# A sixth slot of expert weights, the shared expert inside it, and the first expert unit ahead of its last products

## The chip, the cores and the metric

The kernel runs on one core of one Trainium2 chip. The metric is the device time in microseconds (us) of one execution. All times below are of this one core.

## The reference, cut to what matters

One decoder layer for 256 prompt tokens and 8 sample tokens, 264 tokens in all, model width 1024, everything in fp32. The first half of the layer (an RWKV-7 mixer, a convolution branch, an output projection) is not touched by the change. The second half is a mixture of experts: 64 experts of width 256, of which the router takes 8 for each token, and one shared expert of width 256 that every token goes through.

```python
h = x + mix                                   # mixers, w_out
xf = rmsnorm(h, norm2_g)                      # 264 x 1024
scores = sigmoid(xf @ w_router)               # 264 x 64
gate = top 8 of the biased scores (4 of 8 groups), normalised, times 2.5
routed = sum over e of (silu(xf @ w_gate[e]) * (xf @ w_up[e]) * gate[:, e]) @ w_down[e]
shared = (silu(xf @ ws_gate) * (xf @ ws_up)) @ ws_down
y = rmsnorm(h + routed + shared, normf_g)
```

w_gate, w_up and w_down are 1 MiB for each expert, so 192 matrices of 1 MiB have to be read once; the shared expert's three are 1 MiB each as well.

## The kernel before, in words

After the mixers (until about 440 us) five programs run side by side, one for each engine, and meet at semaphores: `moe_sp` (SyncE issues the weight loads, in order, on one queue), `moe_pe` (TensorE), `moe_act` (ScalarE), `moe_dve` (VectorE) and `moe_pool` (GpSimd, which gathers token rows).

**Weights.** A ring of `NSLOT` = 5 slots at the top of on-chip memory; a slot holds one expert's three matrices. A "load" is one matrix. Expert number n of the order goes to slot n % 5. The shared expert's gate and up matrices are loaded first, into slot 3 (`SHARED_SLOT`), its down matrix into a buffer of its own, `wsd`; expert 3's gate and up are loaded when the shared products that read slot 3 are done (`shg_mm` 4). `moe_sp` (L438 to L474) then goes through the units: after unit u's gate and up products (`h_mm` u+1, here called h1 for unit 0, h4 for unit 3) it issues the gate and up loads of the experts that take the same slots, and after its down products (`yx_mm` u+1) their down loads.

**Units.** The 64 experts are worked through in 26 units, `UNITS = 'PPP' + 'T' + 'TP' * 11`. A P unit has two experts with 64 token slots each, a T unit three: one with 64 slots and two with few tokens, with 32 each. The first six experts are taken as numbered; the others are sorted by their token counts. A unit's 128 token slots are the 128 partitions of its tile `xe`: VectorE compares each token's position in its expert's list with the slot numbers (`match`, L963), TensorE turns that into row numbers (`index`), VectorE hands them over (`fetch_rows`), and GpSimd gathers the rows from DRAM by an indirect DMA (`fetch`, L1173), of 4 KiB for each slot that holds a token; empty slots move nothing. Slots are filled from the first on, so the low partitions of each strip of 64 or 32 are the ones that are filled.

**One unit on TensorE** (L714 to L728): `index(q+3)`; in units 4 to 12 one of the nine pieces of the shared expert's down product, `shared_down` (`DOWN_AT` = 4, `NDOWN` = 9); `gate_up(q)`; `combine(q-1)`, which weighs and adds the results of the unit before; `turn_hidden(q)`; `turn_gates(q)`; `turn(q+1)`, which transposes the gathered rows; `down(q)`. A `shared_down` writes half a PSUM bank, `ps_sd`, that VectorE has to add to `xrow` (`shared_rows`) before the next one may write it, and before `turn_hidden` may write the other half of that bank (`shy_ready`).

**Ahead of unit 0** TensorE interleaves the router's small products with the shared expert's 32 gate and up products (`shared_gate_up`, 128x264 each, k of 8 in four groups), which all come before `gate_up(0)`.

Of the kernel before, what the change touches and what calls it, by code (L numbers as in the profile page):

```python
# [23 lines left out]
ACT = mybir.ActivationFunctionType  # L24
AX = mybir.AxisListType

D = 1024
# [54 lines left out]
def constants():  # L82
# [9 lines left out]
    parts['slot'] = np.tile(np.arange(SLOTS * MAXPASS)[None, :], (128, 1))  # L92
    parts['token'] = p[:, None] + 128 * np.arange(3)[None, :] - NOROW
# [31 lines left out]
def layer_step(nc, A, out, stop=9):  # L125

    ctx = ExitStack()
    with ctx:
# [189 lines left out]
        NSLOT = 5  # L318
        SHARED_SLOT = 3
        NXE, NYE, NIX, NGT = 2, 2, 8, 6  # L320
        ring0 = TOTAL - NSLOT * 3 * 2048
        assert P2.at <= ring0, (P2.at, ring0)
# [7 lines left out]
        scm = E.take(9 * NE)  # L330
        sc, rp, MK = (scm[:, 3 * NE * i:3 * NE * i + 3 * NE].rearrange("p (t e) -> p t e", t=3) for i in range(3))
        PGT = scm[:, 0:NT]
        bi, bm = (E.take(3, NE) for _ in range(2))
# [14 lines left out]
        OHg = E.take(3, 2 * SLOTS)  # L348
# [28 lines left out]
        xeT1 = xeT[0].rearrange("p k n -> p (k n)")[:, 0:KT * SLOTS].rearrange("p (k n) -> p k n", k=KT)  # L377
        hid1 = hid[0][:, 0:2 * SLOTS]
        hT1 = hT[0].rearrange("p j n -> p (j n)")[:, 0:2 * SLOTS].rearrange("p (j n) -> p j n", j=2)
# [50 lines left out]
        DOWN_AT, NDOWN = 4, 9  # L430
# [7 lines left out]
        def moe_sp(sp):  # L438
            for part, n in enumerate(('ws_gate', 'ws_up')):
                load_item(sp, part, SHARED_SLOT, A[n][0])  # L440
            for e in range(3):
                for part in range(3):
                    load_item(sp, part, e, expert_w(part, e))
            load_item(sp, 2, 3, expert_w(2, 3))
# [16 lines left out]
            for u in range(NU_E):  # L461
# [9 lines left out]
                if after:  # L471
                    sp.wait_ge(S['yx_mm'], u + 1)
# [1695 lines left out]
```

## Time and profile before

| | |
|---|---|
| median of 3 runs | 1015.59 us (1015.31 to 1017.05) |
| profiled execution, its own time | 1017.33 us |
| its span, first to last instruction | 1015.5 us |
| mean granted TensorE clock | 0.971 |
| busy: TensorE, its weight loads, VectorE, ScalarE, GpSimd | 92%, 56%, 49%, 23%, 24% |
| read from DRAM | 263.75 MB |
| weight loads of the experts | 192 of 1024 KB |

The span is about 1.8 us shorter than the execution's own time. The 40 slices of the page are 25.4 us each; the expert half begins in the eighteenth. A busy share of the DMA engines near 1.0 means that all 16 of them move data.

### The profile page before, as it was taken

The page shows a single profiled execution, that of the slowest core. Times are in us where ns is not written, and L with a number is a line of the kernel's source. Part 1 is how long each engine was busy: PE and PEld are TensorE (multiplying, and loading weights), DVE is VectorE, ACT ScalarE, POOL GpSimd, SP SyncE. Part 2 cuts the span into 40 slices and gives each one's busy share as a digit, 9 for nine tenths or more (in the row PEclk, how much of TensorE's full clock was granted, in tenths as well). Part 3 has the DMA queues.
Part 4 walks back from the last instruction along what each step waited for, and adds up shares of the span by engine and source line. Part 5 has one row for each costly group of instructions (what it writes and reads, how often), then busy time and mean ns, then how long its engine had stood idle before and what let it go on. Part 6 is the DMA issues. An engine that isn't in the chain of part 4 may idle for free.

```text
span 1015.5 us, 19351 instructions
## 1 busy us (share of the span) xinstructions
PE 931.5 (92%) x7882; PEld 564.9 (56%) x7882; DVE 500.6 (49%) x1040; ACT 232.7 (23%) x483; POOL 243.5 (24%) x281
## 2 busy tenths in 40 slices
PE   4999999999999997779999999999999799899895
PEld 4878877887787777536834344443343234333332
DVE  2148857885787486985623333432323233323225
ACT  3231134113411351254112111111111111111213
POOL 0039904960794099100100000000000000000000
PEclk9999999999999999979999999999999899999989
DMA  8633144214412408139589999999999999999961
GB/s 243 184 125 95 31 125 142 65 44 138 126 55 84 139 2 290 27 140 419 199 361 406 395 419 420 419 420 419 419 420 420 418 415 419 420 414 419 419 282 44
DMA packets 76741, 265.04 MB, mean 261 GB/s; under 512 B 12942, under 2 KB 44240, under 8 KB 51799
## 3 DMA queue, kind: packets, MB, share of 16 engines
q1 hardware_dynamic: 72791, 254.09, 64.5%
q0 software_dynamic: 3856, 9.64, 2.5%
q8 instruction: 65, 1.06, 0.4%
q14 instruction: 29, 0.24, 0.1%
HBM read 263.75 MB, written 5.89 MB: 266 GB/s over the span
## 4 chain that ended last, share of the span: by engine, by line
PE 62%; DMA 23%; DVE 6%; SPq 3%; ACT 3%; issue 2%; DVEq 0%; ACTq 0%
PE bank L1333 60%; DMA big<-in_w_up 22%; SPq L401 2%; ACT big L1630 2%; DMA big<-in_w_in 1%; PE bank L628 1%; DVE big L1920 1%; ACT L1630 1%; DVE big L1977 1%; DVE big L1973 0%; DVE big L897 0%; DVE big L1168 0%; SPq L1228 0%; PE bank L693 0%; DVE big L1983 0%
## 5 line engine op out<-in xcount | busy, mean ns | idle before, releaser
L1333 PE MATMUL bank<-big 64*64 64x64 f32 (+8 forms) x7412 | 872.1, 373 | 61.5 <-DMA big<-in_w_up 27.6
L1333 PEld LDWEIGHTS bank<-big 64*64 64x64 f32 (+4 forms) x7412 | 509.1, 143 | 406.8 <-issue 336.3
L1630 ACT ACTIVATE big<-bank 128x512 f32<-128x512 f32 (+8 forms) x283 | 121.7, 459 | 620.2 <-PE bank L1333 473.7
L1174 POOL DMA_INDIRECT big<-xg,big x26 | 25.9, 995 | 506.4 <-PE bank L628 399.6
L2119 POOL TENSOR_SCALAR big<-big 128x256 f32<-128x256 f32 x120 | 127.0, 1059 | 0.4
L1045 DVE TENSOR_TENSOR big<-big,bank 128x256 f32<-128x256 f32 x26 | 11.0, 422 | 210.3 <-ACT big L1630 210.3
L2131 POOL TENSOR_TENSOR big<-big 128x256 f32<-128x256 f32 x120 | 87.4, 729 | 0.3
L1083 DVE TENSOR_TENSOR big<-big,bank 128x512 f32<-128x512 f32 x104 | 71.5, 688 | 12.7 <-PE bank L1333 11.3
L1920 DVE SCALAR_TENSOR_TENSOR big<-big 128x256 f32<-128x256 f32 x120 | 74.0, 617 | 4.1
L990 DVE TENSOR_SCALAR big<-bank 128x1 uint32<-128x1 f32 x26 | 4.1, 156 | 112.8 <-PE bank L1333 112.5
L1630 ACT ACTIVATE big<-big 128x272 f32<-128x272 f32 (+9 forms) x108 | 49.8, 505 | 42.6 <-DVE big L1855 11.3
L1630 ACT ACTIVATE big<-bank,big 128x272 f32<-128x272 f32 (+2 forms) x53 | 23.8, 475 | 111.6 <-PE bank L1333 111.5
L2115 POOL TENSOR_SCALAR big<-big 128x256 f32<-128x256 f32 x4 | 2.2, 550 | 170.5 <-DVE big L1898 170.5
L1630 ACT ACT_TABLE_LOAD x30 | 38.5, 1283 | 3.8 <-DVE big L912 2.6
L1837 DVE SCALAR_TENSOR_TENSOR big<-bank,big 128x272 f32<-128x272 f32 x26 | 13.0, 498 | 45.5 <-ACT big L1630 45.5
L966 DVE TENSOR_TENSOR big<-big 128x192 f32<-128x192 f32 (+1 forms) x76 | 28.5, 425 | 0.1
L628 PE MATMUL bank<-big 128*128 128x128 f32 x208 | 28.4, 280 | 0.0
L628 PEld LDWEIGHTS bank<-big 128*128 128x128 f32 x208 | 22.3, 141 | 0.5
L1973 DVE TENSOR_TENSOR big<-bank,big 128x512 f32<-128x512 f32 x20 | 13.8, 692 | 16.2 <-PE bank L1333 16.2
L656 PEld LDWEIGHTS bank<-big 128*128 128x128 f32 x52 | 10.1, 195 | 14.1 <-issue 11.9
L1985 DVE TENSOR_TENSOR big<-big,bank 128x512 f32<-128x512 f32 x20 | 13.7, 687 | 4.5 <-PE bank L1333 4.3
L976 DVE TENSOR_TENSOR big<-big 128x192 f32<-128x192 f32 (+1 forms) x38 | 15.4, 431 | 0.9
(156 smaller groups left out, 356.8 us busy)
## 6 DMA issues: line engine op xcount, KB each, us to landing
big<-in_w_gate SPq DMA_DIRECT2D x64, 1024.0 KB, 17.9
big<-in_w_up SPq DMA_DIRECT2D x64, 1024.0 KB, 23.6
big<-in_w_down SPq DMA_DIRECT2D x64, 1024.0 KB, 25.2
big<-in_w_in SPq DMA_DIRECT2D x29, 1024.0 KB, 5.4
big<-in_w_out SPq DMA_DIRECT2D x2, 2048.0 KB, 12.1
big<-in_state_wkv SPq DMA_DIRECT2D x32, 64.0 KB, 2.2
out_wkv_s<-big SPq DMA_DIRECT2D x32, 64.0 KB, 3.9
big<-in_x_prompt SPq DMA_DIRECT2D x2, 512.0 KB, 3.2
```

The costliest lines, as they stand in the source:

```text
L401: sp.dma_start(dst, ap).then_inc(S[('wgu_in', 'wgu_in', 'wd_in')[part] + str(slot)], 16)
L628: ins = nc.tensor.transpose(ps_x[h][:, 128 * (k % 4):128 * (k % 4) + 128], xe[q % NXE][:, 128 * k:128 * k + 128], ident)
L966: ins = v.tensor_tensor(dst[:, :, a:b].rearrange("p t (x n) -> p t x n", x=x), K['slot'][:, first:first + w].unsqueeze(1).unsqueeze(1) .br ...
L976: ins = v.tensor_tensor(view, view, at.unsqueeze(3).broadcast_to([128, 3, x, w]), M)
L1083: note(v.tensor_tensor(x, x, comb_bank(q, n), AD), 'cb_sum')
L1174: pool.indirect_dma_start(out=x[0:n, :], out_offset=None, in_=xg, in_offset=bass.IndirectOffsetOnAxis(ap=idxu[0:n, col:col + 1], axis=0), ...
L1333: return nc.tensor.matmul(out_, lhsT=lhsT, rhs=rhs, start=start, stop=stop)
L1630: return nc.scalar.activation(out_, in_, f, **kw)
L1920: note(v.scalar_tensor_tensor(out=acc, in0=u, scalar=cw, in1=acc, op0=M, op1=AD), 'tap')
L1973: link(v.tensor_tensor(Y_st, bank(0), bc(f'level{m}'), M), 'y_ready')
L2119: note(gp.tensor_scalar(TP[:, w % 3, :], u, cw, None, ALU.mult), 'tapm')
L2131: note(gp.tensor_tensor(acc, acc, TP[:, w % 3, :], ALU.add), 'tapm')
```

## The change

- **Memory.** `NSLOT` is 6 and `SHARED_SLOT` 5. `SLOT_AT` places the slots: 0 to 3 where the old slots 0 to 3 were, 5 where the old slot 4 was, and 4 below all of them, over the end of w_out. The space comes from buffers: `xeT`, `hid` and `hT` are single, `NGT` is 2, `ye[1]` and `xq` lie over `x2T`, `wsd` is the down part of slot 5, `OHg`, `bi` and `bm` share one area.
- **Order of the loads.** Experts 0 to 3 whole; then, after the residual (`h2_ready` 8), the shared gate and up and expert 4; the final norm's row behind these; the shared down after `mk_ready`. After h1: gate and up of experts 6 and 7, then those of expert 5 when the shared products are done; expert 5's down when all nine `shared_down` are done.
- **Order on TensorE.** `gate_up(0)` comes ahead of the last ten shared products. The nine `shared_down` lie in units 0 (pieces 0 to 2), 1 (3 to 7) and 2 (8).
- **Order on VectorE and ScalarE** follows: `fetch_rows(0)` ahead of `order_experts`, `shared_hidden(1)` and `shared_rows` inside `pair(0)` to `pair(2)`.
- **Directions.** A new constant `lane` holds 0 to 63 and then 63 to 0. The second strip of 64 in a P unit and the second strip of 32 in a T unit are filled from the last partition down; the strip of 64 of a T unit is filled upwards in one half of the T units and downwards in the other (`q // 2 % 2`).

```diff
@@ -90,6 +90,8 @@
+    lane = np.arange(SLOTS)
+    parts['lane'] = np.tile(np.concatenate([lane, lane[::-1]])[None, :], (128, 1))
...
-        NSLOT = 5
-        SHARED_SLOT = 3
-        NXE, NYE, NIX, NGT = 2, 2, 8, 6
+        NSLOT = 6
+        SHARED_SLOT = 5
+        SLOT_AT = (1, 2, 3, 4, 0, 5)
+        NXE, NYE, NIX, NGT = 2, 2, 8, 2
         ring0 = TOTAL - NSLOT * 3 * 2048
-        assert P2.at <= ring0, (P2.at, ring0)
+        assert P2.at <= ring0 + 6144, (P2.at, ring0)
...
-        scm = E.take(9 * NE)
+        scm = E.take(15 * NE)
-        bi, bm = (E.take(3, NE) for _ in range(2))
+        bi, bm = (scm[:, 3 * NE * i:3 * NE * i + 3 * NE].rearrange("p (t e) -> p t e", t=3) for i in (3, 4))
...
-        OHg = E.take(3, 2 * SLOTS)
+        OHg = scm[:, 9 * NE:15 * NE].rearrange("p (t n) -> p t n", t=3)
...
-        xeT = [E.take(KT, 2 * SLOTS) for _ in range(2)]
-        hid = [E.take(FE) for _ in range(2)]
-        hT = [E.take(2, 2 * SLOTS) for _ in range(2)]
+        xeT, hid, hT = E.take(KT, 2 * SLOTS), E.take(FE), E.take(2, 2 * SLOTS)
-        ye = [x2p[:, 2, :], E.take(D)]
-        xq = E.take(QD)
-        wsd = E.take(2, D)
-        GT = [x2T.rearrange("p k n -> p (k n)")[:, NT * i:NT * i + NT] for i in range(NGT)]
-        E8 = xeT[1].rearrange("p k n -> p (k n)")[:, 0:8 * NE].rearrange("p (a e) -> p a e", a=8)
+        x2T_flat = x2T.rearrange("p k n -> p (k n)")
+        GT = [x2T_flat[:, NT * i:NT * i + NT] for i in range(NGT)]
+        ye = [x2p[:, 2, :], x2T_flat[:, NGT * NT:NGT * NT + D]]
+        xq = x2T_flat[:, NGT * NT + D:NGT * NT + D + QD]
+        E8 = xeT.rearrange("p k n -> p (k n)")[:, 0:8 * NE].rearrange("p (a e) -> p a e", a=8)
...
-            W_ = Arena(big, ring0 + i * 6144, ring0 + (i + 1) * 6144)
+            W_ = Arena(big, ring0 + SLOT_AT[i] * 6144, ring0 + (SLOT_AT[i] + 1) * 6144)
             slot_w.append((W_.take(2, KT, FE), W_.take(2, D)))
+        wsd = slot_w[SHARED_SLOT][1]
...
-        DOWN_AT, NDOWN = 4, 9
+        NDOWN = 9
...
         def moe_sp(sp):
+            for e in range(4):
+                for part in range(3):
+                    load_item(sp, part, e, expert_w(part, e))
+            sp.wait_ge(S['h2_ready'], 8)
             for part, n in enumerate(('ws_gate', 'ws_up')):
                 load_item(sp, part, SHARED_SLOT, A[n][0])
-            for e in range(3):
-                for part in range(3):
-                    load_item(sp, part, e, expert_w(part, e))
-            load_item(sp, 2, 3, expert_w(2, 3))
-            sp.wait_ge(S['h2_ready'], 8)
+            sp.wait_ge(S['wo_mm'], 3)
             load_item(sp, 0, 4, expert_w(0, 4))
             sp.wait_ge(S['x2_ready'], 3)
-            sp.dma_start(grow, A['normf_g'].rearrange("(a d) -> a d", a=1).partition_broadcast(128)) \
-              .then_inc(S['grow_in'], 16)
             sp.dma_start(xg[0:NP, :].rearrange("(t p) d -> p t d", p=128), x2p[:, 0:2, :]).then_inc(S['x2_out'], 16)
             sp.dma_start(xg[NP:NT, :], x2p[0:NS, 2, :]).then_inc(S['x2_out'], 16)
             load_item(sp, 1, 4, expert_w(1, 4))
+            load_item(sp, 2, 4, expert_w(2, 4))
+            sp.dma_start(grow, A['normf_g'].rearrange("(a d) -> a d", a=1).partition_broadcast(128)) \
+              .then_inc(S['grow_in'], 16)
+            sp.wait_ge(S['mk_ready'], 1)
             sp.dma_start(wsd, A['ws_down'][0].rearrange("(j p) d -> p j d", p=128)).then_inc(S['wsd_in'], 16)
-            sp.wait_ge(S['mk_ready'], 1)
-            load_item(sp, 2, 4, expert_w(2, 4))
-            sp.wait_ge(S['shg_mm'], 4)
-            load_item(sp, 0, 3, expert_w(0, 3))
-            load_item(sp, 1, 3, expert_w(1, 3))
             sp.wait_ge(S['perm_out'], 1)
...
+                if u == 0:
+                    sp.wait_ge(S['shg_mm'], 4)
+                    for part in range(2):
+                        load_item(sp, part, SHARED_SLOT, expert_w(part, SHARED_SLOT))
                 if after:
                     sp.wait_ge(S['yx_mm'], u + 1)
                 for n in after:
                     load_item(sp, 2, n % NSLOT, expert_w(2, which.pop(n + NSLOT)))
+                if u == 1:
+                    sp.wait_ge(S['shd_mm'], NDOWN)
+                    load_item(sp, 2, SHARED_SLOT, expert_w(2, SHARED_SLOT))
...
             shared_gate_up(0, 0)
-            shared_gate_up(0, 1, 0, 2)
             pe.wait_ge(S['mk_ready'], 1)
...
-            shared_gate_up(0, 1, 2, 4)
+            shared_gate_up(0, 1, 0, 5)
...
-                if 0 < q + 1 - DOWN_AT < NDOWN:
-                    pe.wait_ge(S['shy_ready'], q + 1 - DOWN_AT)
-                elif q + 1 - DOWN_AT == NDOWN:
+                if q < 3:
+                    pe.wait_ge(S['shy_ready'], (2, 6, 8)[q])
+                if q == 2:
                     pe.wait_ge(S['shs_ready'], 6)
...
-                if q == 0:
-                    pe.wait_ge(S['shh_ready'], 2)
...
-                note(ins, 'yx_mm')
+                    if q == 1:
+                        if h == 1:
+                            note(ins, 'yx_mm')
+                        shared_down(6 + h)
+                if q != 1:
+                    note(ins, 'yx_mm')
 
             index(0)
             turn_choice()
-            shared_gate_up(0, 1, 4, KT)
+            shared_gate_up(0, 1, 5, KT)
             index(1)
             permute()
-            shared_gate_up(1, 0)
+            shared_gate_up(1, 0, 0, 4)
+            turn(0)
             index(2)
-            turn(0)
-            shared_gate_up(1, 1)
+            shared_gate_up(1, 0, 4, 6)
             pe.wait_ge(S['perm_out'], 1)
...
-                if DOWN_AT <= q < DOWN_AT + NDOWN:
-                    shared_down(q - DOWN_AT)
+                if 0 < q < 3:
+                    shared_down(3 if q == 1 else 8)
                 gate_up(q)
-                if q:
-                    combine(q - 1)
+                if q == 0:
+                    shared_gate_up(1, 0, 6, KT)
+                    shared_gate_up(1, 1)
+                    turn(1)
+                    shared_down(0)
+                    turn_gates(0)
+                    shared_down(1)
+                    turn_hidden(0)
+                    down(0)
+                    shared_down(2)
+                    continue
+                if q == 1:
+                    shared_down(4)
+                combine(q - 1)
+                if q == 1:
+                    shared_down(5)
...
-            act.wait_ge(S['shg_mm'], 3)
-            note(fn(sgs[:, 1, :], ps_sh[1][:, 0:NT], ACT.Sigmoid), 'shs_ready')
-
...
-                        wait(act, 'h_mm', q - 1)
-                    note(fn(xeT[q % 2][:, 4 * h:4 * h + 4, :].rearrange("p k n -> p (k n)"), ps_x[h][:, :], ACT.Copy),
+                        wait(act, 'h_mm', q)
+                    note(fn(xeT[:, 4 * h:4 * h + 4, :].rearrange("p k n -> p (k n)"), ps_x[h][:, :], ACT.Copy),
...
-                wait(act, 'htr_mm', q - 1)
-                note(fn(hid[q % 2], ps_gu[q % 2][:, 0:FE], ACT.Sigmoid), 'sig_ready')
-                wait(act, 'yx_mm', q - 1)
-                note(fn(hT[q % 2].rearrange("p j n -> p (j n)"), ps_ht[:, 0:FE], ACT.Copy), 'ht_ready')
...
-                if q == DOWN_AT + NDOWN - 1:
+                if q == 2:
                     act.wait_ge(S['shd_mm'], NDOWN)
...
                 sigma(q)
+                if q == 0:
+                    act.wait_ge(S['shg_mm'], 3)
+                    note(fn(sgs[:, 1, :], ps_sh[1][:, 0:NT], ACT.Sigmoid), 'shs_ready')
+                    turned(1)
                 hidden_turned(q)
-                if q + 1 < NU_E:
+                if 1 <= q < LAST:
                     turned(q + 1)
                 store(q)
...
-                return [(0, SLOTS, SLOTS, 0, choice(q)[:, :, what, n:n + 1]),
+                return [(0, SLOTS, SLOTS, SLOTS * (q // 2 % 2), choice(q)[:, :, what, n:n + 1]),
                         (SLOTS, 2 * SLOTS, STRIP, STRIP, choice(q)[:, :, what, n + 1:n + 3])]
...
-                                          K['slot'][:, first:first + w].unsqueeze(1).unsqueeze(1)
-                                          .broadcast_to([128, 3, x, w]),
+                                          K['lane'][:, first:first + b - a].rearrange("p (x n) -> p x n", x=x)
+                                          .unsqueeze(1).broadcast_to([128, 3, x, w]),
                                           at.unsqueeze(3).broadcast_to([128, 3, x, w]), ALU.is_equal)
...
-            def order_experts():
...
                 v.tensor_copy(ccol, ps_pos[:, 256:257])
+
+            def order_experts():
+
                 link(v.tensor_scalar(below, keyr, keyc, None, ALU.is_lt), chain)
...
             onehot(0)
+            count_keys()
+            fetch_rows(0)
             order_experts()
             onehot(1)
-            v.memset(xq, 0.0)
...
                 if q + 3 < NU_E:
@@ -1051,12 +1078,28 @@
                 if q + 4 < NU_E:
                     onehot(q + 4)
                 gates(q)
-                if DOWN_AT <= q < DOWN_AT + NDOWN:
-                    shared_rows(q - DOWN_AT)
+                if q == 1:
+                    shared_rows(3)
+                if q == 2:
+                    shared_rows(7)
+                    shared_rows(8)
                 hidden(q)
-                if q:
-                    add_late(q - 1)
+                if q == 0:
+                    shared_hidden(1)
+                    v.memset(xq, 0.0)
+                    shared_rows(0)
+                    take_gates(0)
+                    shared_rows(1)
+                    shared_rows(2)
+                    return
+                if q == 1:
+                    shared_rows(4)
+                add_late(q - 1)
+                if q == 1:
+                    shared_rows(5)
                 take_gates(q)
+                if q == 1:
+                    shared_rows(6)
 
...
-            fetch_rows(0)
-            onehot(2)
             shared_hidden(0)
             fetch_rows(1)
+            onehot(2)
             take_order()
             onehot(3)
             fetch_rows(2)
-            shared_hidden(1)
             pair(0)
```

## Rows read from the trace of the kernel before

**Rows 1.** The page: DMA busy tenths in 40 slices; GpSimd's queue (packets, MB, share).

```profile
DMA  8633144214412408139589999999999999999961
...
q0 software_dynamic: 3856, 9.64, 2.5%
```

**Rows 2.** Windows: busy time of each engine, then clock, DMA share and GB/s.

```profile
core 0: us, PE busy (x) PEld busy (x) DVE busy (x) ACT busy (x) POOL busy (x), PEclk, DMA share, GB/s
492.00:500.00 8.00, 7.88 (x46) 6.49 (x45) 6.22 (x26) 0.39 (x1) 2.14 (x2) 1.00 0.28 84
500.00:506.00 6.00, 6.00 (x35) 5.31 (x34) 0.49 (x2) 1.48 (x3) 0.99 (x1) 1.00 0.12 32
...
564.00:568.00 4.00, 4.00 (x13) 1.91 (x13) 3.51 (x7) 0.13 (x1) 0.00 (x0) 1.00 0.81 281
...
600.00:975.00 375.00, 347.86 (x2073) 143.26 (x2069) 114.97 (x258) 57.31 (x118) 17.80 (x18) 0.95 1.01 419
```

**Rows 3.** Timeline of SyncE's queue: start us, duration us, the issue.

```profile
446.92 0.36 SPq L401 DMA_DIRECT2D big<-in_ws_gate  x1
...
474.35 0.33 SPq L401 DMA_DIRECT2D big<-in_w_gate  x1
...
488.11 0.33 SPq L401 DMA_DIRECT2D big<-in_w_down  x1
506.66 0.33 SPq L401 DMA_DIRECT2D big<-in_w_gate  x1
...
514.34 0.33 SPq L401 DMA_DIRECT2D big<-in_w_gate  x1
...
521.21 0.83 SPq L401 DMA_DIRECT2D big<-in_w_down  x2
...
546.48 0.33 SPq L401 DMA_DIRECT2D big<-in_w_gate  x1
...
563.74 0.33 SPq L401 DMA_DIRECT2D big<-in_w_gate  x1
```

**Rows 4.** The tail of the stream: windows, columns as in Rows 2.

```profile
974.00:990.00 16.00, 15.57 (x99) 6.50 (x93) 5.21 (x10) 2.94 (x6) 0.00 (x0) 1.00 0.49 205
976.00:978.00 2.00, 2.00 (x6) 0.87 (x5) 1.90 (x4) 0.00 (x0) 0.00 (x0) 1.00 0.88 365
```

**Rows 5.** The chain that ended last, from the last weights: start us, us, what.

```profile
944.63 7.10 PE bank L1333 x32
...
957.05 27.53 DMA big<-in_w_up
...
984.72 11.28 PE bank L1333 x48
```

**Rows 6.** The same chain over the router and units 0 to 4.

```profile
483.94 8.34 PE bank L1333 x54
...
492.39 0.88 PE bank L1333 x6
...
503.05 11.27 PE bank L1333 x54
...
515.69 0.50 PE bank L656 x2
...
552.10 15.50 PE bank L1333 x102
...
569.23 16.55 PE bank L1333 x122
```

**Rows 7.** Landing times of the gate loads (tile in_w_gate).

```profile
DMA to landing us min/median/max: 4.9/17.9/22.1
```

**Rows 8.** Landing times of the gathers (line 1174).

```profile
DMA to landing us min/median/max: 3.3/8.5/9.9
```

**Rows 9.** VectorE by shape, 505 to 570 us: busy us, mean ns, idle before.

```profile
L966 DVE TENSOR_TENSOR big<-big 128x384 f32<-128x384 f32 x5 | 2.7, 552 | 0.0
...
L1046 DVE TENSOR_TENSOR big<-big,bank 128x256 f32<-128x256 f32 x4 | 1.7, 422 | 0.1
```

More of the change, by code:

```diff
@@ L376, in layer_step @@
         xe1, ye1, oh1 = xe[0], ye[0], OH[0][:, :, 0:SLOTS]
-        xeT1 = xeT[0].rearrange("p k n -> p (k n)")[:, 0:KT * SLOTS].rearrange("p (k n) -> p k n", k=KT)
-        hid1 = hid[0][:, 0:2 * SLOTS]
-        hT1 = hT[0].rearrange("p j n -> p (j n)")[:, 0:2 * SLOTS].rearrange("p (j n) -> p j n", j=2)
+        xeT1 = xeT.rearrange("p k n -> p (k n)")[:, 0:KT * SLOTS].rearrange("p (k n) -> p k n", k=KT)
+        hid1 = hid[:, 0:2 * SLOTS]
+        hT1 = hT.rearrange("p j n -> p (j n)")[:, 0:2 * SLOTS].rearrange("p (j n) -> p j n", j=2)
         for n in """wgu_in wd_in""".split():
@@ L642, in gate_up @@
                         ins = mm(bank[lo:lo + w, :].rearrange("p (a f) -> p a f", a=2),
-                                 xeT[q % 2][:, k, lo:lo + w], slot_w[n % NSLOT][0][:, :, k, :],
+                                 xeT[:, k, lo:lo + w], slot_w[n % NSLOT][0][:, :, k, :],
                                  k == 0, k == KT - 1)
@@ L650, in turn_hidden @@
                 wait(pe, 'ht_ready', q)
-                if 0 < q + 1 - DOWN_AT < NDOWN:
-                    pe.wait_ge(S['shy_ready'], q + 1 - DOWN_AT)
-                elif q + 1 - DOWN_AT == NDOWN:
+                if q < 3:
+                    pe.wait_ge(S['shy_ready'], (2, 6, 8)[q])
+                if q == 2:
                     pe.wait_ge(S['shs_ready'], 6)
                 for j in range(2):
-                    ins = nc.tensor.transpose(ps_ht[:, 128 * j:128 * j + 128], hid[q % 2][:, j:FE:2], ident)
+                    ins = nc.tensor.transpose(ps_ht[:, 128 * j:128 * j + 128], hid[:, j:FE:2], ident)
                 note(ins, 'htr_mm')
@@ L812, in sigma @@
                 act.wait_ge(S['h_mm'], q + 1)
-                wait(act, 'htr_mm', q - 1)
-                note(fn(hid[q % 2], ps_gu[q % 2][:, 0:FE], ACT.Sigmoid), 'sig_ready')
+                wait(act, 'htr_mm', q)
+                note(fn(hid, ps_gu[q % 2][:, 0:FE], ACT.Sigmoid), 'sig_ready')
             def hidden_turned(q):
                 act.wait_ge(S['htr_mm'], q + 1)
-                wait(act, 'yx_mm', q - 1)
-                note(fn(hT[q % 2].rearrange("p j n -> p (j n)"), ps_ht[:, 0:FE], ACT.Copy), 'ht_ready')
+                wait(act, 'yx_mm', q)
+                note(fn(hT.rearrange("p j n -> p (j n)"), ps_ht[:, 0:FE], ACT.Copy), 'ht_ready')
             def store(q):
@@ L1010, in shared_rows, with count_keys @@
                 sums[1] += 1
-            def order_experts():
+            def count_keys():
                 link(v.tensor_tensor(keyr, ps_pos[:, 192:256], K['count_row'], M), chain)
@@ L1038, in moe_dve @@
             onehot(0)
+            count_keys()
+            fetch_rows(0)
             order_experts()
             onehot(1)
-            v.memset(xq, 0.0)
             def hidden(q):
                 dve.wait_ge(S['sig_ready'], q + 1)
-                link(v.tensor_tensor(hid[q % 2], hid[q % 2], ps_gu[q % 2][:, 0:FE], M), chain)
-                note(v.tensor_tensor(hid[q % 2], hid[q % 2], ps_gu[q % 2][:, FE:2 * FE], M), 'hid_ready')
+                link(v.tensor_tensor(hid, hid, ps_gu[q % 2][:, 0:FE], M), chain)
+                note(v.tensor_tensor(hid, hid, ps_gu[q % 2][:, FE:2 * FE], M), 'hid_ready')
             def pair(q):
```

2 lines of the change are left out of this document (1 added, 1 removed).

## The prediction

> **What bounds the kernel now.** I read the page's slices first, then windows over the stretch that they point at, then SyncE's timeline, and last the chain that ended last. In the slices the DMA engines are mostly idle for the first eighteen, full in the nineteenth, half idle in the twentieth (482 to 508 us), and full from the twenty-second to the thirty-eighth [rows 1]. From 600 to 975 us they move 419 GB/s at a share of 1.01, while TensorE has 27 us to spare [rows 2]. So the expert half is a stream of weights, and what counts is when its last gate and up matrices land. The chain says so at its end: the last up load lands at 984.58, 31 us before the end of the span, and `gate_up` of the last unit starts 0.14 us later [rows 5].
>
> One load is 1.0486 MB, at 419 GB/s 2.50 us. The 264 x 8 = 2112 gathered rows of 4 KiB are 8.65 MB of the 9.64 MB on GpSimd's queue [rows 1]: 0.54 MB or 20.6 us for each of the 16 engines, if they share it evenly. They don't. From 974 to 990 us the mean share is 0.49 [rows 4]: the engines run dry one after the other, and the last is 16 x 0.51 = 8.1 us behind the mean. A load has landed when its slowest engine has, so these 8.1 us are paid.
>
> Two holes cost the stream time before: after the load at 488.11 it waits for the shared products, until the issue at 506.66 (shares of 0.28 and 0.12 between 492 and 506), and once more until h1 at 514.34 [rows 2, 3]. From then on TensorE sets the pace for a while: a P unit takes about 17.3 us, its six loads 15.0. The stream runs dry just before h4 (563.74), where a share of 0.81 shows the restart [rows 2, 3]. Unit 3 has three experts, nine loads or 22.5 us, and the backlog grows from there. **So the end follows from h4.** Check: at h4 the loads of experts 11 to 63 are still to be issued, 53 x 3 = 159; the last up matrix is the 157th, since two down loads follow it. It lands 420.8 us later: 157 x 2.50 = 392.5, 2.4 of latency (below), and 25.9 for the gathers on the slowest engine, where the even 20.6 and the 8.1 give 28.7, less what belongs to the units before.
>
> **Ahead of h1.** The shared gate and up matrices were first in the queue (446.92) and are now the thirteenth and fourteenth loads, issued behind `h2_ready` at 474.35 [rows 3]. Fourteen loads from 446.92 are 35.0 us, 481.9; a load that finds an idle queue lands 4.9 - 2.5 = 2.4 us later than its bytes take [rows 7], so 484.3, and one engine a little behind may make it 486. The shared products started at 483.94 [rows 6]. Bounds 0.4 and 2; I take 1.4 late. One 128x264 product: 11.27 us are eight of them, one `index` (0.88) and a `gate_up` (7.10) [rows 5, 6], so (11.27 - 0.88 - 7.10)/8 = 0.41 us. The block of 8.34 us held 12 products (4.9) and 3.4 us of counting with waits; now it has 13, so `index(0)` comes 1.4 late, perhaps 1.6. Behind it stood 20 products ahead of h1 and now stand 9: 11 x 0.41 = 4.5 us less. GpSimd gets the first rows' numbers as before, and 3.3 us of landing [rows 8], behind the shared down load in the queue, put them at about 500.5, where `turn(0)` comes to stand (+0.1). **h1: -4.5 + 1.4 + 0 to 0.3 = 3.0 us earlier, 511.3.** By then the same 15 expert loads and three shared ones are done as before (the eighteen end at about 499), so the holes shrink from two to one of 12 us, for nothing but these 3.0.
>
> **From h1 to h4.** All that follows is TensorE's path, with no other cover:
> - The ten moved shared products, 4.1 us. They hide the wait for ScalarE and VectorE between 514.32 and 515.69 [rows 6], 1.4 us: net 2.7.
> - Nine `shared_down` now lie ahead of h4; before, none (they began in unit 4). One is two 128x256 products, 0.85 us; the two T units' chains, 15.50 without and 16.55 with one, give 1.05 with its wait [rows 6]. 9 x 0.85 = 7.6.
> - Their waits. Pieces 0 and 1 share a bank, so piece 1 waits for VectorE's add of 0.42 us [rows 9], after `turn_gates` 0.3; `turn_hidden(0)` waits for `take_gates(0)` and the next add, 0.6, and `down(0)` now stands right behind ScalarE's copy, 0.5, because `turn(1)` went ahead; `turn_hidden(1)` waits for the last add of the combine and piece 5's, 0.5. Piece 8 waits for piece 7's add, and VectorE's order puts `fetch_rows(5)`, a onehot, and match and weigh of `gates(2)` first, three of 0.55 and more [rows 9]: 2.4. Sum 4.3; bounds 2 (if VectorE finds the time earlier) and 8.
> - Single `xeT`, `hid`, `hT` cost nothing: each new wait (`h_mm` q, `htr_mm` q, `yx_mm` q) is for work that TensorE has finished when ScalarE gets there, since ScalarE takes `sigma`, `hidden_turned` and `turned` in that order already. `NGT` 2 waits for a combine one unit back, done too.
>
> Sum 2.7 + 7.6 + 4.3 = 14.6, less the 3.0: **h4 comes 11.6 us later, 575.3.** Does the stream run dry by then? h3 is 546.48 + 11.6 = 558.1; its six loads (15.0), a gather (0.8) and half of the 2.4 of latency take 17.0, until 575.1. Just. So h4 can lose at most about 1.5 us before h3 sets the end instead.
>
> **What the sixth slot gives at h4.** Experts 0 to 11 are issued by then, not 0 to 10: 156 loads are left, not 159. But the end of the order shifts too. Before, unit 23 (experts 57 and 58) freed the slots of 62 and 63 together: four gate and up loads, then two down loads, which `down` of the last unit doesn't need for another 11 us [rows 5]. Now it frees only 63's slot: the last gate and up loads are the 155th of 156. So 155 against 157, not 156 against 159: **5.0 us earlier.** Nothing behind them changes: the last 31 us stay.
>
> **Directions.** The first strip of a P unit still fills from below and the second now from above; T units alternate. Low partitions of one half no longer always get the extra rows, but P units still load one end of each half. I take half of the 8.1: **4.0 us**; bounds 0 and 7.
>
> The Trainium skill ("DMA: Bandwidth & Descriptors", The descriptor swizzle) assigns partitions to engines by engine = 8 x (partition >> 6) + ((partition >> 2) & 7). With the token counts that the reference's inputs give (11 to 61 for the sorted experts), my estimate from that rule is 168 rows for the fullest engine from unit 4 on before, 142 after, and 118 in the mean; 26 rows at 4 KiB and a sixteenth of 419 GB/s are 4.1 us, and the sum would be the same within 0.1. The rule's 50 rows above the mean are 7.8 us, beside the 8.1 that the tail shows.
>
> `lane` adds 64 KB to a constants load at the start, 0.16 us of the stream there, beside idle engines. The final norm's row and the token rows move by two loads; both are long there when needed.
>
> **Sum.** +11.6 - 5.0 - 4.0 = **+2.6 us**. Against the profiled execution's 1017.3 that is 1019.9; that execution lies 1.7 above the median of 1015.59, so I say **1018.2** for the median. Its own range is 1016 to 1021.
>
> **Rivals.** 0.2% is 2.0 us, about what a measurement of this kernel can tell from no change.
> - *Forecast* (h4 sets the end): 0.44, of which 0.28 is beyond +2.0 and 0.16 within.
> - *The stream runs from h1 on without a hole* (faster). Then the last gate and up loads, the 176th behind h1 and not the 175th, come 3.0 earlier and 2.5 later, 4.0 earlier by directions: -4.5, 1011.1. With the hole of 564 closed, -5. For it: two more loads are out between h1 and the down products. Against: a P unit's 15.9 us of traffic against 17.3 on TensorE, and 12 us more on TensorE. It decides from h4 less than 7.0 us late (7.0 - 9.0 = -2.0). 0.16.
> - *The directions even out nearly all*: 4.0 more, -1.4, 1014.2, or fewer waits, no change. For: the ramp is the whole 8.1. Against: the P units. 0.19, with 0.17 within 0.2%.
> - *The directions do nothing* (the slowest engine is slow for another reason): +6.6, 1022.2. The even ramp down from 976 (0.88) speaks against one odd engine [rows 4]. 0.10.
> - *The waits in units 0 to 2 cost 8 us*: +6.3, 1021.9. 0.11.
>
> Faster 0.16 + 0.02 = 0.18; within 0.16 + 0.17 = 0.33; slower 0.28 + 0.10 + 0.11 = 0.49. The range has to reach both signs: 1010.5, below the faster rival, to 1022.5, above the two slow ones.
>
> **What would show it.** In SyncE's timeline h1 at 511, h4 at 575 (under 571 if the faster rival holds), and one hole in the stream before h1 instead of two. In the windows, shares under 0.9 around 531, 543, 553 to 559. In the chain, the last up load at 987 and 31 us behind it. At the tail, a ramp half as long as 8 us. TensorE's chain should show 0.5 to 2.5 us of VectorE in units 0 to 2. The forecast falls if TensorE's work from h1 to h4 grows by less than 10 or more than 18 us, or if the ramp doesn't shrink.

## The result and the profile after

The changed kernel takes 1028.8 us, the median of 4 runs (1026.58 to 1031.14). The kernel before took 1016.32 in the same comparison (4 runs, 1015.31 to 1017.48). The ratio is 1.012, with a 95% interval from 1.0103 to 1.0136. The forecast was 1018.2, between 1010.5 and 1022.5: the direction came true, the size lies outside the range. The profiled execution took 1026.58, its span is 1024.8 (before 1015.5), and its mean granted clock 0.967.

The page of the changed kernel, its row of DMA slices and GpSimd's queue; they answer to [rows 1]:

```profile
DMA  8633134115312407159587999999999999999961
...
q0 software_dynamic: 3856, 9.64, 2.5%
```

The gathers are the same. The stream of weights is full up to the thirty-eighth slice, as before, but only from the twenty-third on and not from the twenty-second. Windows of the changed kernel, columns as in [rows 2]:

```profile
480.00:488.00 8.00, 4.03 (x20) 3.16 (x19) 7.24 (x55) 1.98 (x6) 0.00 (x0) 0.84 1.00 401
488.00:496.00 8.00, 8.00 (x55) 7.10 (x53) 2.04 (x8) 0.39 (x1) 0.00 (x0) 0.95 1.02 420
...
504.00:512.00 8.00, 8.00 (x42) 3.52 (x41) 1.73 (x6) 0.00 (x0) 0.99 (x1) 1.00 0.10 26
...
544.00:552.00 8.00, 6.81 (x33) 3.29 (x31) 1.57 (x5) 2.08 (x4) 0.99 (x1) 1.00 0.72 273
552.00:560.00 8.00, 7.01 (x38) 2.22 (x40) 2.12 (x4) 1.50 (x4) 0.00 (x0) 0.79 0.81 334
560.00:568.00 8.00, 8.00 (x40) 3.50 (x37) 4.25 (x8) 0.77 (x2) 0.00 (x0) 1.00 0.48 186
...
600.00:975.00 375.00, 348.09 (x2051) 142.54 (x2049) 115.28 (x259) 58.43 (x119) 18.79 (x19) 0.95 1.01 419
...
984.00:1000.00 16.00, 16.00 (x98) 6.22 (x92) 5.21 (x10) 2.94 (x6) 0.00 (x0) 1.00 0.39 161
```

From 600 us on the rate is the same 419 GB/s at the same share. Two things are new. Between 480 and 496, and again between 552 and 560, TensorE's granted clock is below 1.00, each time behind a stretch in which it was not busy throughout (4.03 of 8 us, 6.81 of 8). And the stream, which ran dry only just before h4 in the kernel before, stands half idle from 560 to 568. SyncE's timeline of the changed kernel, beside [rows 3]:

```profile
446.74 0.36 SPq L403 DMA_DIRECT2D big<-in_w_gate  x1
...
472.53 0.33 SPq L403 DMA_DIRECT2D big<-in_ws_gate  x1
...
512.76 0.35 SPq L403 DMA_DIRECT2D big<-in_w_gate  x1
...
525.91 0.86 SPq L403 DMA_DIRECT2D big<-in_w_down  x2
535.84 0.33 SPq L403 DMA_DIRECT2D big<-in_w_gate  x1
...
562.89 0.33 SPq L403 DMA_DIRECT2D big<-in_w_gate  x1
...
580.15 0.33 SPq L403 DMA_DIRECT2D big<-in_w_gate  x1
```

h1 is 512.76, 1.6 us earlier than before. But the issue behind `h2_ready`, 472.53 here, was already 1.8 us earlier (474.35), so from that issue to h1 it is 40.2 us, before 40.0. h2, h3 and h4 are 535.84, 562.89 and 580.15: h4 is 16.4 us later than the 563.74 of before, where 11.6 was forecast. The chain that ended last, over the router and units 0 to 3 of the changed kernel:

```profile
472.90 12.31 DMA big<-in_ws_up
...
485.25 11.14 PE bank L1374 x62
...
541.87 0.43 DVE big L1029
...
551.01 1.02 DVE big L989 x3
...
552.52 0.43 DVE big L1029
552.99 13.90 PE bank L1374 x64
```

The landing of the shared up matrix holds TensorE, from 481.2 to 485.25, and the wait ahead of piece 8 does it once more, until 552.99. The chain's end, beside [rows 5]:

```profile
947.04 27.88 DMA big<-in_w_up
974.92 0.14 issue
975.06 13.75 PE bank L1374 x80
...
990.43 14.78 PE bank L1374 x80
```

Here the chain differs in kind from [rows 5]: the last DMA in it is that of the weights of the last unit but one (24), not of the last unit. The last block, 14.78 us, holds the end of unit 24's work and the `gate_up` of the last unit. By itself that `gate_up` took 11.28 [rows 5], so it begins at 990.43 + 14.78 - 11.28 = 993.9, behind TensorE's own work. Before it began at 984.72. From there both kernels take 31 us more (30.9 and 30.8), so the 9.3 us between the spans are the 9.2 between the two starts. The tail of the stream of the changed kernel, in windows, is beside [rows 4]:

```profile
990.00:992.00 2.00, 2.00 (x20) 0.74 (x22) 0.91 (x2) 1.09 (x2) 0.00 (x0) 1.00 0.39 164
992.00:994.00 2.00, 2.00 (x22) 0.46 (x16) 0.00 (x0) 0.00 (x0) 0.00 (x0) 1.00 0.15 61
```

With the share of 0.39 from 984 to 1000 the engines idle 9.8 us in the mean, of which 6 lie behind 994, where the stream is over: the last engine is 3.8 us behind the mean, not 8.1.

### The profile page after: what moved, and what is told of

It reads as the page before. It is cut to its first block, busy times and chain, and to the rows that moved or that the text cites. A ratio compares the mean times of both kernels' runs of the same rounds, so it can differ in the third digit from the quotient of the medians.

```text
span 1024.8 us, 19351 instructions
## 1 busy us (share of the span) xinstructions
PE 935.9 (91%) x7882; PEld 566.3 (55%) x7882; DVE 501.5 (49%) x1040; ACT 232.7 (23%) x483; POOL 243.5 (24%) x281
## 4 chain that ended last, share of the span: by engine, by line
PE 63%; DMA 24%; DVE 6%; ACT 2%; SPq 2%; issue 2%; DVEq 0%
PE bank L1374 61%; DMA big<-in_w_up 22%; ACT big L1671 2%; SPq L403 2%; DMA big<-in_ws_up 1%; DMA big<-in_w_in 1%; PE bank L633 1%; DVE big L1961 1%; DVE big L2018 1%; ACT L1671 1%; DVE big L2014 0%; DVE big L1209 0%; SPq L1269 0%; PE bank L701 0%; PE bank L661 0%
## 5 line engine op out<-in xcount | busy, mean ns | idle before, releaser
L1374 PEld LDWEIGHTS bank<-big 64*64 64x64 f32 (+5 forms) x7412 | 510.4, 144 | 415.4 <-issue 336.8
L1671 ACT ACT_TABLE_LOAD x30 | 38.5, 1283 | 3.8 <-DVE big L935 2.6
```

Of the source, the lines that this page charges most:

```text
L1374: return nc.tensor.matmul(out_, lhsT=lhsT, rhs=rhs, start=start, stop=stop)
L1671: return nc.scalar.activation(out_, in_, f, **kw)
```

## The experiments

Each ratio is to runs of the kernel before on the same chip, whose median lay between 1016.3 and 1017.2. The last five columns are of the one profiled execution: "start" is the issue behind `h2_ready`, just ahead of the part in which the change alters TensorE's order; "last unit" is the start of its `gate_up`, from the chain as above. From there to the end of the span it is 30.7 to 30.9 us in all but `last_up_late`.

The start column differs by up to 2.8 us where the change leaves TensorE's work alone (472.06 to 474.83 with the change, 473.39 to 474.35 without). So a difference of that size in h1, h4, last unit or span alone says little. Counted from the start, the executions agree: to h1 it is 39.97 to 39.99 us in `before`, `dirs_only` and `last_up_late`.

| kernel | median us | ratio to before (95%) | start | h1 | h4 | last unit | span |
|---|---|---|---|---|---|---|---|
| before | 1016.32 | | 474.35 | 514.34 | 563.74 | 984.7 | 1015.5 |
| after | 1028.8 | 1.012 (1.0103 to 1.0136) | 472.53 | 512.76 | 580.15 | 993.9 | 1024.8 |
| dirs_only | 1014.92 | 0.9979 (0.9967 to 0.9991) | 473.66 | 513.64 | 563.05 | 980.6 | 1011.4 |
| after_straight | 1031.48 | 1.0139 (1.0114 to 1.0163) | 474.83 | 515.13 | 582.58 | 998.5 | 1029.3 |
| down_at_0 | 1020.93 | 1.004 (1.0026 to 1.0054) | 473.46 | 514.57 | 567.16 | 988.3 | 1019.1 |
| last_up_late | 1018.99 | 1.0022 (1.0008 to 1.0036) | 473.39 | 513.36 | 562.77 | 986.3 | 1020.0 |
| ws_first | 1025.2 | 1.0092 (1.0069 to 1.0114) | 473.08 | 510.88 | 578.27 | 991.7 | 1022.6 |
| piece8_late | 1024.02 | 1.0076 (1.0054 to 1.0098) | 472.87 | 512.82 | 577.26 | 991.1 | 1021.9 |
| both_waits | 1023.34 | 1.0074 (1.0049 to 1.0099) | 474.42 | 512.79 | 577.22 | 989.8 | 1020.6 |
| five_in_ring | 1031.4 | 1.0152 (1.0129 to 1.0174) | 472.06 | 512.15 | 579.71 | 997.4 | 1028.2 |
| after_again | 1027.23 | 1.0093 (1.0077 to 1.011) | 474.24 | 514.53 | 581.99 | 996.1 | 1026.8 |
| busy_wait | 1025.5 | 1.009 (1.0066 to 1.0114) | 472.86 | 511.47 | 580.03 | 992.2 | 1023.0 |
| no_pieces | 1013.36 | 0.9957 (0.994 to 0.9973) | 473.96 | 513.67 | 567.30 | 981.0 | 1011.8 |
| busy_last | 1026.58 | 1.0106 (1.0083 to 1.0129) | 473.28 | 513.19 | 580.63 | 992.7 | 1023.5 |

### The directions alone, and everything but the directions

`dirs_only` is the kernel before with the constant `lane` and these lines:

```diff
-                return [(0, SLOTS, SLOTS, 0, choice(q)[:, :, what, n:n + 1]),
+                return [(0, SLOTS, SLOTS, SLOTS * (q // 2 % 2), choice(q)[:, :, what, n:n + 1]),
...
-                                          K['slot'][:, first:first + w].unsqueeze(1).unsqueeze(1)
-                                          .broadcast_to([128, 3, x, w]),
+                                          K['lane'][:, first:first + b - a].rearrange("p (x n) -> p x n", x=x)
+                                          .unsqueeze(1).broadcast_to([128, 3, x, w]),
```

> The kernel before with the slot directions of the change alone (five slots, everything else as before). Theory (a load lands with its slowest engine, and the directions take about half of its lag): the stream's ramp at the end shortens from 8.1 us behind the mean to about 4, and the kernel gets 3 to 4.5 us faster than before, about 1012.3. Rival (the slowest engine is slow for another reason than its gathered rows): ramp and time unchanged, within 1 us.

`after_straight` is the changed kernel with the same lines turned back.

> The changed kernel with all slots filled upwards, as before. Theory: 4 us slower than the changed kernel, about 1032 to 1033, with h4 unchanged at 580 and a ramp of 8 us. Rival: as the changed kernel, since its last unit is bound by TensorE at half clock and not by the landing: 1 us or less.

In `after_straight` the landing does set the start of the last unit. The chain of its end:

```profile
970.58 27.83 DMA big<-in_w_up
...
998.55 11.28 PE bank L1374 x48
```

Its last up matrix lands at 998.41, 415.8 us behind its h4. With the directions that interval is 411.9 (`busy_last`, below): 3.9 us, the forecast's 4.0. In `dirs_only` the last unit starts 417.5 us behind h4, before 421.0: 3.4 us. The time gets less of it: 1.7 us in the median of `dirs_only` (11 runs against 23 of before; by the interval 0.9 to 3.4), whose profiled execution was the fastest of the 11. `after_straight` lies 14.8 us above before, the changed kernel 12.5 and, in `after_again`, 10.1. In both kernels with directions TensorE is still busy with unit 24 when the last weights land, which takes 0.5 us in `dirs_only`; the rest of the gap between 3.4 and 1.7 stays open. The chain of `dirs_only` ends with the same two blocks as that of the changed kernel:

```profile
962.71 12.77 PE bank L1335 x80
...
977.10 14.78 PE bank L1335 x80
```

`dirs_only` beats both kernels.

### The pieces early, and the end of the order

`down_at_0` is the kernel before with the nine pieces in units 0 to 8:

```diff
-        DOWN_AT, NDOWN = 4, 9
+        DOWN_AT, NDOWN = 0, 9
```

> The kernel before with the nine pieces of the shared down product one in each of units 0 to 8 and not 4 to 12, so that four of them lie ahead of h4. Theory (the end follows from h4, where the stream runs dry): h4 moves by 4 x 1.05 = 4.2 us, and the last up load and the end by as much, +3.5 to +5. Rival (the stream is one queue that is full from h1 on, and TensorE's pace in units 0 to 3 is hidden): no change, within 1 us.

From the start to h4 it is 93.7 us, before 89.4: four pieces cost 4.3 us, 1.08 each. Counted the same way the last unit begins 4.5 us later, and the median is 4.3 above that of before (1016.66). A delay of h4 is paid in full.

`last_up_late` is the kernel before with the gate and up loads of expert 63 behind the down load of 62, where six slots put them:

```diff
                 for n in after:
+                    if u == 23 and n + NSLOT == NE - 1:
+                        continue
...
+                    if u == 23 and n + NSLOT == NE - 2:
+                        for part in range(2):
+                            load_item(sp, part, (n + 1) % NSLOT, expert_w(part, which[n + 1 + NSLOT]))
```

> The kernel before, but of the last six loads the gate and up of expert 63 come behind the down load of expert 62, as the sixth slot makes it: the same loads, the last up load one place later. Theory: +2.5 us, one load. Rival (the last unit starts when TensorE has finished the one before it, so that one load's delay is hidden): 0 to 1 us.

```profile
961.91 24.29 DMA big<-in_w_up
986.20 0.14 issue
986.33 14.06 PE bank L1338 x48
```

The last up matrix lands 423.4 us behind h4, before 420.8: one load, 2.6 us. The median rises by 2.3. The profiled execution pays 2.8 more, since these 48 products, behind a wait of 3.5 us for the weights, took 14.06 us and not 11.28.

### The two waits of the changed kernel

`ws_first` loads the three shared matrices first, as before, and expert 3 behind the residual:

```diff
-        SLOT_AT = (1, 2, 3, 4, 0, 5)
+        SLOT_AT = (1, 2, 3, 5, 0, 4)
...
-            for e in range(4):
+            for part, n in enumerate(('ws_gate', 'ws_up')):
+                load_item(sp, part, SHARED_SLOT, A[n][0])
+            for e in range(3):
```

> The changed kernel with the places of slots 3 and 5 exchanged, so that the shared expert's three matrices are loaded first of all, as before, and expert 3 behind the residual. Theory (TensorE's wait for the late shared matrices, 481 to 485 us, costs itself and a stretch at the half clock behind it): the shared products start at 483.9 at full clock, h1 comes 2.5 to 4 us earlier than the changed kernel's 512.8, and the kernel is that much faster: about +9 us on the kernel before. Rival (the wait is only made up by VectorE's routing, which bounds the block): h1 within 0.5 us, no gain.

`piece8_late` puts the ninth piece behind `gate_up(2)`:

```diff
-                if 0 < q < 3:
-                    shared_down(3 if q == 1 else 8)
+                if q == 1:
+                    shared_down(3)
...
+                if q == 2:
+                    shared_down(8)
                 combine(q - 1)
```

> The changed kernel with the ninth piece of the shared down product behind unit 2's gate and up products and not ahead of them. Theory (TensorE stood 2.2 us for VectorE's add of piece 7 and then ran a stretch at the half clock): h3 4 to 5 us earlier than 562.9, h4 4 earlier than 580.2, the end 3.5 to 4.5 us earlier: about +8.5 us on the kernel before. Rival (the wait only moves to the next place, turn_hidden of unit 2, which needs the same add and four copies): less than 1 us.

`both_waits` has the edits of both.

> The changed kernel with both edits, the shared matrices first and piece 8 late. Theory: the gains add up, 6.5 to 8 us, since both lie on TensorE's path to h4 (about 573): about +5 us on the kernel before. Rival (by then h3 or the queue set the end and not h4): 4 to 5 us, no more than the larger of the two.

From the start (the issue behind `h2_ready`) to h4 it is 107.6 us in the changed kernel (107.8 in `after_again`), 105.2 in `ws_first`, 104.4 in `piece8_late` and 102.8 in `both_waits`: gains of 2.4, 3.2 and 4.8 us. The absolute h4 of `both_waits` hides this, since its start is 1.9 us later than that of the changed kernel. From h1 to h4 the two parts separate cleanly: 67.4 us in the changed kernel and in `ws_first`, 64.4 in `piece8_late` and in `both_waits`. So the two gains add up but for 0.8 us. In the medians they are 8.8, 7.6 and 6.9 us above before, against 12.5 and 10.1 for the changed kernel, and there the intervals are too wide to tell. `piece8_late` has no drop of the clock from 552 to 560; `ws_first` still has one, 0.79 from 488 to 496, behind two short waits for ScalarE and VectorE (0.83 and 0.39 us), so its gain is not that of a full clock. The chain of `both_waits` shows part of the missing 0.8:

```profile
496.92 5.12 DMA big<-xg,big
502.05 0.04 issue
502.09 1.09 PE bank L636 x8
503.18 14.06 PE bank L1379 x68
```

`turn(0)` waits 0.45 us for the gathered rows, which it does neither in `ws_first` nor in the changed kernel.

### Six slots or five in the ring

`five_in_ring` keeps the changed kernel's layout and order, but the sixth slot holds the shared expert alone:

```diff
-        NSLOT = 6
+        NSLOT = 5
...
-                if u == 0:
-                    sp.wait_ge(S['shg_mm'], 4)
-                    for part in range(2):
-                        load_item(sp, part, SHARED_SLOT, expert_w(part, SHARED_SLOT))
```

> The changed kernel with the sixth slot used by the shared expert alone: the experts go round five slots as before, everything else is as changed. Theory (the sixth slot is worth three loads at h4 and gives one back at the end, 5.0 us): 5 us slower than the changed kernel, about +17 us on the kernel before, h1 and h4 unchanged (512.8, 580.2). Rival (the slot is worth nothing once the stream is the bound): as the changed kernel, +12.

From h4 to the end of the span it is 448.5 us, in the changed kernel 444.6: the slot in the ring gives 3.8 us, less than the 5.0 of two loads. In both TensorE's unit 24 stands in front of the last unit, so the landing's own gain isn't seen here. Its median is 15.0 us above before, against 12.5 and 10.1.

### What TensorE's waits cost behind them

`after_again` is the changed kernel unchanged, beside the next two on one chip.

> The changed kernel once more, beside the next two. If the stretches at the half clock behind TensorE's waits (485 and 553 us) differ from execution to execution, h1 and h4 of this one differ from 512.8 and 580.2 by one or two us, and the time lies 9 to 14 us over the kernel before.

`busy_wait` gives TensorE five products of 512 columns, never read, in front of its wait for the shared weights:

```diff
+            for _ in range(5):
+                mm(ps_pos[:, :], ident, x2p[:, 0, 0:512])
             pe.wait_ge(S[f'wgu_in{SHARED_SLOT}'], 32)
```

> The changed kernel with five extra products (128x128 by 512 columns, results never read) where TensorE waits for the shared matrices from 481 to 485 us: the wait stays, TensorE is busy in it. Theory (the wait costs also what the half clock behind it takes): no stretch at the half clock near 485, h1 1.7 to 3.4 us earlier than in the changed kernel beside it. Rival (the block behind it is bound by VectorE's routing, whatever the clock): h1 unchanged within 0.5 us.

```profile
480.00:488.00 8.00, 8.00 (x37) 5.23 (x38) 7.10 (x54) 2.31 (x7) 0.00 (x0) 1.00 0.99 400
488.00:496.00 8.00, 8.00 (x58) 7.12 (x57) 3.13 (x13) 0.73 (x2) 0.00 (x0) 1.00 1.02 421
...
552.00:560.00 8.00, 8.00 (x38) 2.39 (x32) 1.22 (x1) 1.51 (x4) 0.00 (x0) 0.65 0.69 261
```

The clock stays at 2.4 GHz from 480 to 496, and h1 follows the start after 38.6 us, where the two executions of the changed kernel show 40.2 and 40.3, and the five others that are the same up to h1 39.7 to 40.3. So the low clock costs 1.6 us there, 1.1 at the least. From h1 to h4 this execution takes 68.6 us, where the six others with piece 8 in its place take 67.4 to 67.6: behind the same 2.2 us wait for VectorE the clock was 0.57 for 8 us, in the six 0.79. Whether the extra products have a part in that, one execution can't show.

`no_pieces` leaves the nine `shared_down`, their additions and their waits out, so the shared expert is missing from its output:

```diff
             def shared_down(n):
-
-                if n == 0:
...
+                pass
```

> The changed kernel without the shared expert's down product: its nine pieces, their additions and their waits are left out, so the shared expert is missing in the output. Theory (the pieces and their waits are what makes h4 late): h1 as in the changed kernel, h4 12 to 15 us earlier, about 567, and the end 10 to 13 us earlier, near the kernel before; once h4 is that early the stream may be full already at h3 or h1, so less than all of it arrives. Rival (the sixth slot's buffers or the order around unit 0 cost the time): h4 no more than 8 us earlier.

From h1 to h4 it takes 53.6 us, the kernel before 49.4 and the changed kernel 67.4. Its window and its chain:

```profile
530.00:560.00 30.00, 29.29 (x144) 12.73 (x140) 10.22 (x21) 5.52 (x12) 1.98 (x2) 1.00 1.01 420
```

```profile
954.63 26.27 DMA big<-in_w_up
...
981.03 11.27 PE bank L1346 x48
```

This splits the stretch from h1 to h4. TensorE's busy time in it, before, in the changed kernel, in `piece8_late` (all nine pieces, no low clock) and in `no_pieces`:

```profile
514.34:563.74 49.40, 48.05 (x273) 19.95 (x273) 14.94 (x34) 8.96 (x19) 2.97 (x3) 1.00 0.98 397
512.76:580.15 67.39, 63.31 (x341) 29.74 (x340) 20.55 (x46) 10.70 (x24) 2.97 (x3) 0.97 0.84 337
512.82:577.26 64.44, 61.77 (x341) 29.71 (x340) 20.11 (x46) 10.70 (x24) 2.96 (x3) 1.00 0.86 343
513.67:567.30 53.63, 52.44 (x293) 23.70 (x292) 16.07 (x37) 9.21 (x20) 2.98 (x3) 1.00 0.99 408
```

Of the 18.0 us that the changed kernel takes more than before, the moved products are 52.44 - 48.05 = 4.4, the nine pieces 61.77 - 52.44 = 9.3 (1.04 each), the low clock 63.31 - 61.77 = 1.5, and the rest, 2.7, is idle time: 67.39 - 63.31 = 4.1 against 49.40 - 48.05 = 1.35.

In `no_pieces` the stream is full from 530 on. h4, 3.6 us later than before, no longer sets the end: by h4 alone the span would be 3.6 - 8.9 = 5.3 below that of before, and it is 3.7 below.

`busy_last` gives TensorE seven products in front of its wait for unit 24's weights:

```diff
                     wait(pe, 'hid_ready', q)
+                    for _ in range(7 if q == LAST - 1 else 0):
+                        mm(ps_gu[q % 2][:, 0:320], ident, K['slot'])
```

> The changed kernel with seven more products (128x128 by 320 columns, never read) in front of TensorE's wait for the weights of the last unit but one, so that TensorE computes instead of idling there. Theory (the last unit begins when TensorE is through with the unit before it, 1.6 us late since that unit began at half clock behind TensorE's wait, and its weights lay there 1.7 us earlier, at about 992.2 by the windows): the granted clock stays at 1.0 from 970 to 990 us, the last unit but one takes 17.3 us and not 18.8 from its first product to its last, and the span is 1.5 to 1.7 us below that of the changed kernel for the same h4 (the issue behind unit 3); the median 1 to 2 us below the changed kernel's. Rival (the landing of the last up matrix sets the start of the last unit): the clock may stay up, but the last unit starts where it did, and span less h4 stays within 0.5 us of the changed kernel's 444.6.

The window of `busy_last`, that of the changed kernel, and then the chain of `busy_last`:

```profile
974.00:982.00 8.00, 8.00 (x69) 3.09 (x71) 0.00 (x0) 0.00 (x0) 0.00 (x0) 1.00 1.02 419
```

```profile
974.00:982.00 8.00, 6.94 (x43) 2.00 (x46) 0.00 (x0) 0.00 (x0) 0.00 (x0) 0.60 1.02 419
```

```profile
966.28 26.27 DMA big<-in_w_up
992.55 0.14 issue
992.68 11.27 PE bank L1376 x48
```

The landing is back in the chain, 411.9 us behind h4, and TensorE waited 1.05 us for it. The span less h4 is 442.9 us, in the changed kernel 444.6: 1.8 us, as the theory had it. Without the extra products it differs from execution to execution: 444.8 in `after_again`, 444.3 in `ws_first`, 444.6 in `piece8_late`, 443.4 in `both_waits`, 443.0 in `busy_wait`. The timed runs don't resolve it: the ratio's interval overlaps that of `after_again`.

The wait itself is not new. The kernel before had it too, and the low clock behind it:

```profile
965.78 13.31 PE L1333 MATMUL bank<-big 128*32 128x512 f32 x80 [4.68 <-DMA big<-in_w_up]
...
984.72 11.28 PE L1333 MATMUL bank<-big 128*64 128x512 f32 x48 [0.43 <-DMA big<-in_w_up]
```

There TensorE was through with unit 24 just 0.43 us before the last weights landed. With the landing 8.9 us earlier behind h4, the same work came out last.

## Why the prediction was off

**What bounds the kernel: right.** The chain still runs from h4 to the last weights. `down_at_0` shows that a delay of h4 is paid in full, and `no_pieces` where this ends.

**What h4 doesn't set: right.** Forecast were 5.0 us earlier for the order of the loads and 4.0 for the directions, 9.0 together. From h4 to the last landing it is 411.9 us (`busy_last`, where the chain shows it) against 420.8: 8.9. Of the directions' part, 3.9 at the landing, the timed runs show 1.7 in `dirs_only`. The Trainium skill ("DMA: Bandwidth & Descriptors", The descriptor swizzle) gave 142 - 118 = 24 rows for the fullest engine, my estimate from its formula 3.8 us; the trace agrees with its 3.8 behind the mean.

**The faster rival: its mechanism exists, its condition was not met.** It needed h4 less than 7.0 us late. With h4 3.6 late and h1 0.7 early, `no_pieces` shows no hole at h4 and a shorter time, though without the shared expert's down product.

**The step that failed: TensorE's path up to h4.** Forecast was h1 at 511.3, 3.0 us earlier, then 14.6 us more work and waits, h4 11.6 later. Counted from the start (the issue behind `h2_ready`), h1 is 0.2 later (0.3 in `after_again`), then come 18.0 more (67.4 against 49.4), and h4 is 18.2 later (18.4). Those 18.0 lie at the bound of 18 that the forecast itself named as a sign against it. By terms:
- *Ahead of h1*, forecast 3.0 earlier, measured 0.2 and 0.3 later. The landing that the shared products start with was well forecast in absolute time, 485.3 against 485.21. But it hangs on the first load's issue (38.5 us behind it in both executions of the changed kernel) and not on `h2_ready`, so that the start is 1.8 us earlier in this execution gives nothing: the shared products begin 12.7 us behind it, before 9.6, so 3.1 us later (2.5 in `after_again`), where 1.4 was forecast. From the landing to h1 the forecast has 26.0 us; measured are 27.5 and 28.2. That is the clock behind the wait for the landing, put at nothing in the forecast: 1.6 us by `busy_wait`.
- *The moved products*, forecast 4.1, less 1.4 for a wait that they hide. Measured 4.4.
- *The pieces*, forecast 9 x 0.85 = 7.6, measured 9.3. The forecast's own rows gave 1.05 for one piece; it put the difference down to a wait, but it is work: 1.04 each here, 1.08 in `down_at_0`.
- *The waits*, forecast 4.3, or 2.9 net of the 1.4. TensorE idles 4.1 us, 2.7 more than before, so this was right: 2.2 for piece 8, 1.3 for two `turn_hidden`, 0.5 for ScalarE's copy.
- *The low clock behind piece 8's wait*, forecast nothing, measured 1.5.

**The end.** "Nothing behind them changes" was right of the 31 us, and wrong of what starts them. With the last landing at 580.15 + 411.9 = 992.1 the last unit could have begun at 992.2; TensorE was through with unit 24 at 993.9. It had waited 4.7 us for unit 24's weights and began that unit at the lower clock, as it did before, where 0.43 us were to spare; `busy_last` takes this away and gets the 1.8 back. So of the gain of 8.9 us, 1.7 were not paid out (2.0 in `after_again`).

**The sum.** 16.4 - 8.9 + 1.7 = 9.2, the difference between the starts of the last unit in the two profiled executions; the forecast had 11.6 - 9.0 = 2.6. The 1.8 us by which the start came earlier in this one is luck as far as the table shows, since the ranges of the two kinds of kernel overlap there. Counted from the start it is 18.2 - 8.9 + 1.7 = 11.0, and 11.5 in `after_again`, beside the 12.5 and 10.1 by which the medians lie above those of before. Of the 8.4 us between 11.0 and 2.6, some 3.1 are clock (1.6 and 1.5), 1.7 the pieces' size, 1.7 the end, and most of the rest the later start of the shared products.

In the changed kernel three of TensorE's gaps (at 481, 551 and 970 us) are each followed by a fall of the clock to its 1.2 GHz level: it is 0.50 from 486 to 488, from 553.76 to 555.76 and from 975 to 979 us. By the runs above that costs 1.5 to 1.8 us each time. The Trainium skill ("TensorE: Matmul & The Clock Gate", HAM oscillation) describes this for loops that wait for a DMA: the wait throttles the engine, and the work behind it starts cold. The trace agrees for the two waits for weights, and the 2.2 us wait for VectorE does the same here. The forecast priced each wait at its own length and left this rule out.

## What to carry to other kernels

Where TensorE's path sets the time, a wait can cost its own length and a stretch of slow products behind it: price both, and look whether a wait of before already paid it. When a row gives the price of one step, here 1.05 us for a piece, take it before a lower one from a count of products. Work that is moved ahead of the point from which a full stream follows is paid in full, even if the engine has 27 us to spare behind that point. When a transfer gets faster, read which engine is next in line, here TensorE 1.7 us behind. Test the parts of a change alone: one small part of this one (`dirs_only`) was the only one that made the kernel faster. And compare single executions from an event that lies just ahead of the change, not from the start of the span: by absolute times the two edits of `both_waits` seem not to add up, counted from the issue behind `h2_ready` they nearly do.

## What was not expected of the hardware

- TensorE at work on products that nobody reads, during a wait, made the real ones behind it faster: 1.6 us in `busy_wait`, 1.8 in `busy_last`, each read from one execution.
- Half the lag of the slowest DMA engine (8.1 us to 3.8) goes away by filling the gathered strips from the other end, with the same rows and bytes.
- The cost of the clock behind one and the same wait is not fixed: behind piece 8's wait of 2.2 us it was 0.79 for 8 us in six executions and 0.57 in `busy_wait`, 1.1 us more.
